# All warming matmuls taken out of a single-core transformer trunk in fp32

## What is computed

```python
for i in range(2):
    sh1, sc1, g1, sh2, sc2, g2 = split(silu(c) @ ada_w[i] + ada_b[i], 6)
    hm = rms_norm(x, gain[i, 0]) * (1 + sc1) + sh1
    mix = attention(hm) if i == 0 else mamba2_mixer(hm)
    x = x + g1 * mix
    hf = rms_norm(x, gain[i, 1]) * (1 + sc2) + sh2
    ffn = swiglu(hf) if i == 0 else moe_swiglu(hf)
    x = x + g2 * ffn
```

## Time and profile before

| | |
|---|---|
| median of 3 runs | 1727.41 us |
| the three runs | 1726.98, 1727.41, 1732.47 us |
| profiled execution | 1734.41 us |
| its span | 1732.6 us |
| granted TensorE clock, mean over the span | 0.983 |
| TensorE busy (share of the span) | 1661.9 us (96%) |
| VectorE busy | 1395.3 us (81%) |
| ScalarE busy | 1094.1 us (63%) |
| read from HBM | 495.78 MB, 287 GB/s over the span |

### The profile page before, as it was taken

One profiled execution on the slowest core, in us unless ns is written; L12 is line 12 of the kernel. 1 busy time (PEld: TensorE's weight loads), 2 busy tenths in 40 slices (PEclk: granted clock), 3 DMA queues, 4 the chain that ended last, 5 costly groups with the idle time before them and its releaser, 6 DMA issues.

```text
span 1732.6 us, 25093 instructions
## 1 busy us (share of the span) xinstructions
PE 1661.9 (96%) x7709; PEld 1308.4 (76%) x7709; DVE 1395.3 (81%) x1557; ACT 1094.1 (63%) x1333; POOL 0.2 (0%) x4
## 2 busy tenths in 40 slices
PE   7888999999999989899999999999999999999996
PEld 2735777778778768588888888888888888888884
DVE  2565887776567685799898998998998998998996
ACT  2544444433365663577777777777877787787773
POOL 0000000000000000000000000000000000000000
PEclk9989999999999989899999999999999999999998
DMA  9667597876545215299999998998999999999991
GB/s 358 239 236 273 218 358 274 279 257 217 175 125 179 85 39 157 68 372 374 346 354 365 346 361 335 383 358 329 387 361 341 364 365 337 362 375 342 354 375 72
DMA packets 206214, 497.94 MB, mean 287 GB/s; under 512 B 18155, under 2 KB 20508, under 8 KB 205992
## 3 DMA queue, kind: packets, MB, share of 16 engines
q1 hardware_dynamic: 206120, 496.91, 79.8%
HBM read 495.78 MB, written 1.07 MB: 287 GB/s over the span
## 4 chain that ended last, share of the span: by engine, by line
PE 86%; DVE 5%; ACT 3%; issue 2%; DVEq 0%; ACTq 0%
PE acc L1565 25%; PE acc L1572 25%; PE acc L1566 24%; PE xb L1854 2%; PE xb L1820 2%; PE xb L1602 1%; PE acc L1550 1%; PE acc L1665 1%; DVE cv L1332 1%; DVE w_lo L926 1%; PE acc L1948 1%; PE xb L1650 1%; PE xb L1843 1%; PE xb L1844 1%; PE xb L1872 0%
## 5 line engine op out<-in xcount | busy, mean ns | idle before, releaser
L926 DVE TENSOR_TENSOR w_lo<-raw,w_hi 128x1024 fp32r<-128x1024 f32 x832 | 993.7, 1223 | 167.3 <-ACT w_hi L575 142.3
L575 ACT ACTIVATE w_hi<-raw 128x1024 fp32r<-128x1024 f32 x832 | 864.8, 1058 | 306.3 <-PE acc L1572 283.0
L1565 PE MATMUL acc<-w_hi,g_hi 128*128 128x512 f32 x896 | 354.3, 395 | 1.0 <-DVE g_lo L1511 1.0
L1566 PE MATMUL acc<-w_hi,g_lo 128*128 128x512 f32 x896 | 349.0, 390 | 0.0
L1572 PE MATMUL acc<-w_lo,g_hi 128*128 128x512 f32 x896 | 276.6, 390 | 0.2 <-DVE w_lo L926 0.2
L1572 PEld LDWEIGHTS acc<-w_lo,g_hi 128*128 128x128 f32 x896 | 168.0, 188 | 36.3 <-DVE w_lo L926 0.8
L1565 PEld LDWEIGHTS acc<-w_hi,g_hi 128*128 128x128 f32 x896 | 168.3, 188 | 34.5 <-issue 1.1
L1565 PE MATMUL acc<-w_hi,a_hi 128*128 128x512 f32 x464 | 185.2, 399 | 8.9 <-DVE a_lo L976 4.6
L1566 PEld LDWEIGHTS acc<-w_hi,g_lo 128*128 128x128 f32 x896 | 168.4, 188 | 33.2
L1566 PE MATMUL acc<-w_hi,a_lo 128*128 128x512 f32 x464 | 181.7, 392 | 0.0
L1565 PE MATMUL acc<-w_hi,e_hi 128*128 128x512 f32 x448 | 177.9, 397 | 0.0
(11 more groups left out here) (254 smaller groups left out, 1469.2 us busy)
## 6 DMA issues: line engine op xcount, KB each, us to landing
raw<-in_moe_w_gu SPq DMA_DIRECT2D x448, 512.0 KB, 6.0
raw<-in_moe_w_down SPq DMA_DIRECT2D x224, 512.0 KB, 5.3
raw<-in_ada_w SPq DMA_DIRECT2D x96, 512.0 KB, 6.1
raw<-in_ffn_w_gu SPq DMA_DIRECT2D x56, 512.0 KB, 5.8
raw<-in_ssm_w_in SPq DMA_DIRECT2D x40, 512.0 KB, 4.7
raw<-in_ffn_w_down SPq DMA_DIRECT2D x28, 512.0 KB, 5.0
raw<-in_ssm_w_out SPq DMA_DIRECT2D x16, 512.0 KB, 4.2
raw<-in_attn_w_qkv SPq DMA_DIRECT2D x12, 512.0 KB, 15.1
```

Of the source, the lines that this page charges most:

```text
L575: act.activation(w_hi[:, w % SPLIT, :], raw[:, no % RAW, :], ACT.Copy).then_inc(hi_ready, 1)
L926: dve.tensor_tensor(w_lo[:, w % SPLIT, :], raw[:, no % RAW, :], r32(w_hi[:, w % SPLIT, :]), ALU.subtract).then_inc(raw_used, 1)
L1565: pe.matmul(o, l_hi[:, k, rows_], hi[:, col:col + HALF], start=new, stop=False)
L1566: pe.matmul(o, l_lo[:, k, rows_], hi[:, col:col + HALF], start=False, stop=False)
```

## The change

All six counts become 0, so `keep_warm` issues nothing in any of the eight places. TensorE's program has 3008 rows in place of 3016; the waits for PSUM buffers that stand ahead of `keep_warm`, and the programs of the other engines, are the same.

```diff
-WARM_FIRST, WARM_NORM, WARM_SSD, WARM_Y, WARM_MASK, WARM_ROUTE = 3, 9, 5, 4, 2, 3
+WARM_FIRST, WARM_NORM, WARM_SSD, WARM_Y, WARM_MASK, WARM_ROUTE = 0, 0, 0, 0, 0, 0
```

## The result

The changed kernel took 1750.24 us in the median of 4 runs (1747.68 to 1752.08), against 1729.87 us for the kernel before (1726.98 to 1732.47, 4 runs). The ratio is 1.0117, with a 95% interval of 1.0099 to 1.0136: slower by 1.2%. The profiled execution took 1752.08 us.

A forecast was written before the change was run, and what follows sets the result against it. TensorE, nearly always granted full clock, was taken to bound the kernel. Terms 5.6 + 2.0 + 3.8 + 1.1 + 0.9 + 4.6 = 18.0 us, put on the 1727.4 median, gave 1745.4 us, range 1736 to 1754.

The forecast's parts named there:

- What is saved: At all emptied waits: removed passes free no time, except 0.4 us at the routing, where they delay the gather.
- The unit price: At each cold start: 4.2 us at half clock once dense products begin, a loss of 2.1 us.
- norm1, norm2: Transposes at half delay the first product by 0.7 us, then a 2.1 us cold start: 2.8 us each.
- norm0: Clock falls near the wait's end, transposes still run in full: 2.0 us lost, bounds 0 and 3.1.
- The scan: First unit runs at half throughout, 4.7 us more, 0.9 made up: 3.8 us, bounds 1.7 and 4.7.
- Gated norm: Transposes 0.7 us later, then 2.1, but 1.7 already lost before: 1.1 us, bounds 0 and 2.8.
- norm3: First transposes 0.7 us later, clock already at half afterwards, 0.2 added: 0.9 us, bounds 0 and 1.5.
- Routing: Gather at half, 2.5 us including the 0.4 saved, then first expert's cold start 2.1: 4.6 us.
- The smaller price: Whole kernel: clock returns faster or lost time is made up, 8.5 us more, 1736 us; chance 0.12.
- nothing: Whole kernel: clock does not fall or returns within the first product, 1727 us; chance 0.07, shared with a cancellation.
- stay cold: Scan: small products at half never bring the clock back, all eight units run at half, 1773 us; chance 0.05.
- Rival 3: Norm waits and routing: passes begun at low clock last twice as long, so removal is faster, 1724 or 1716; chance 0.04.

The follow-up runs named there:

- Parts and whole: Four runs against the kernel before, passes removed at the norms, scan, mask and routing, norm0 and gated norm: 1.0033, 1.0023, 1.0026, 1.0032; whole change 1.0117.
- the two light forms: Kernel before with its 44 warming matmuls using only 8 identity columns (ratio 0.9993), or only 8 rows of identity and constants (ratio 1.0209).
- 3.5 alone: Kernel before without warming passes at norm1, norm2 and norm3 only: 1737.19 against 1729.97 us, ratio 1.0033.
- 2.0 alone: Kernel before without warming passes at norm0 and ahead of the gated norm's transposes only: 1735.65 against 1729.26 us, ratio 1.0032.
- 5.0 alone: Kernel before without warming passes ahead of the first scan unit only: 1735.08 against 1729.97 us, ratio 1.0023.
- the run with 8 rows: Kernel before with warming matmuls using 8 rows of identity and constants, 8 partitions read, 128 written: 1766.04 against 1729.26 us, ratio 1.0209.
- the last version of all: Kernel before plus warming matmuls: three behind norm3's first transposes, two behind the gated norm's, three ahead of the last scan unit: 1728.74 against 1731.63 us, ratio 0.9986.
- The run with twelve passes: Kernel before with twelve warming matmuls in place of nine at norm1, norm2 and norm3: 1737.79 against 1731.63 us, ratio 1.0053.
- that with five: Kernel before with five warming matmuls in place of nine at norm1, norm2 and norm3: 1739.24 against 1731.63 us, ratio 1.0043.

## Why the prediction was right

The forecast was 18.0 us more, 1745.4 in the median; measured were 20.4 us between the medians and 1750.24, inside the range of 1736 to 1754. Part of the distance lies in the reference: with one more run the median of before became 1729.87. The mechanism and the total were right; the terms were less so, and their errors cancel in part. Step by step:

- **What bounds.** TensorE, and its clock: right. Parts and whole add up, and the two light forms show that the clock is the cause.
- **What is saved: nothing, and 0.4 at the routing.** Right for the norms. At the routing 0.2 us was saved behind `pick`, but the five counting products (lines 1991 to 1995) that make VectorE's input stand 0.43 us apart instead of 0.22 with the clock down, which makes `pick` 1.0 us later. The prediction had priced the gather and the tiles at half and passed over these.
- **The unit price, 4.2 us at half behind the first dense product, 2.1 lost.** Right in the mean, but not the same at each place. The clock behind the first dense product of norm0, norm2, the gated norm and the first expert:

```profile
39.81:46.20 6.39, 6.39 (x20) 5.17 (x21) 2.32 (x3) 0.14 (x1) 0.00 (x0) 0.53 1.04 391
459.09:462.50 3.41, 3.41 (x9) 2.72 (x10) 2.42 (x4) 0.00 (x0) 0.00 (x0) 0.54 1.03 422
655.90:660.10 4.20, 4.20 (x10) 3.37 (x11) 4.20 (x5) 0.00 (x0) 0.00 (x0) 0.50 0.64 219
741.43:745.70 4.27, 4.27 (x10) 3.37 (x11) 4.27 (x5) 2.00 (x2) 0.00 (x0) 0.52 0.40 124
```

  With norm1 this makes about 6.0, 6.0, 3.1, 4.2 and 4.1 us at half, 4.7 in the mean. From the first product to the first behind the second transposes it took 6.41, 6.46, 5.08 and 5.62 us at norm0, norm1, norm2 and the gated norm, where 3.63 or 3.64 is the time in full; so 2.8, 2.8, 1.4 and 2.0 us were lost, and 1.9 in the first expert's first two tiles: 2.2 in the mean. That one price would fit both long and short ones was a simplification, and that they average out is luck.
- **norm1, norm2: 2.8 each.** Norm1 3.6 (3.5 alone); norm2 2.0, of which 0.7 is the transposes, as forecast, and 1.4 the products.
- **norm0: 2.0.** 2.7, and 2.0 alone.
- **The scan: 3.8.** 4.2, and 5.0 alone, of which 0.8 belongs to the last unit. The argument that the small products at half don't bring the clock back and that one whole unit is paid was right: the third unit is 4.9 us later relative to the first. Of that 0.5 is made up by the last unit and 0.7 by the gated norm, close to the 0.9 forecast.
- **Gated norm: 1.1.** 0.8.
- **norm3: 0.9.** 0.2. The transposes cost 0.7, but the router's last products ran in full in this execution, which gave most of it back.
- **Routing: 4.6.** 5.1, made up of 0.8 from the counts to the gather (1.0 lost at the counts, 0.2 saved), 2.9 from there to the first tile, and 1.4 up to the ninth tile; of the 1.9 us lost in the first two tiles the kernel before lost 0.5 itself a little later, in part waiting for `w_lo`.
- **The rivals.** The smaller price, nothing, and faster are out by the interval. The scan did not stay cold: its second unit was at full pace. Rival 3 did not occur here, but its mechanism is real, as the run with 8 rows shows.
- **The rule** of under 1% for coming up to the full clock, from the Trainium skill, page "TensorE: Matmul & The Clock Gate", section "What's actually happening", does not hold for this change as a whole: 1.17%, though the interval, 0.99 to 1.36, just touches 1. Read as the price of one ramp it agrees: the largest single place cost 5.1 us, 0.3%.

The forecast for the profiled execution, 1752.4, met 1752.08 by cancellation, which is luck: norm0, norm1, the scan and the routing came out 2.4 us above their terms together, and norm2, the gated norm and norm3 1.8 below; the rest of the table is 0.9 shorter, nearly all of it in the stretch up to the end.

The scatter between executions, 4 to 10 us in every kernel here, comes in good part from half-clock stretches between the first product of the query/key/value projection and that of the output projection. Over that part, the profiled execution of the kernel before and that of the last version of all, which issue the same instructions up to there:

```profile
39.91:150.84 110.93, 93.62 (x509) 53.91 (x509) 68.45 (x123) 51.05 (x125) 0.00 (x0) 0.92 0.71 256
```

```profile
40.18:143.81 103.63, 86.08 (x508) 51.28 (x508) 68.41 (x123) 51.02 (x125) 0.00 (x0) 1.00 0.74 270
```

7.3 us lie between them, at a mean clock of 0.92 and 1.00. The run with twelve passes, the same up to there as well, took 106.97 us at 0.97, that with five 112.68 at 0.91. So single profiled executions can't be compared by their whole spans, which is why the parts above are compared stretch by stretch. What makes the clock fall there in one execution and not in the next stays open.

## What to carry to other kernels

Count TensorE's idle time on a chain over other engines twice: once for itself, and once for the half clock that may follow it, which here cost 2 to 5 us at most of the waits, and under 1 at the gated norm and norm3, where the kernel before had part of the loss already. It was paid nearly in full because TensorE bounded the next stage. A wait has to be filled almost to its end: with nine matmuls the clock held over the 0.7 to 0.95 us left idle ahead of norm2, the gated norm and the scan; with five, and 3.26 us left at norm1, it did not, and the whole time was not told from that with none; twelve cost their overhang. And look at what small serial work stands between the wait and the dense products (transposes, counts, gathers), for it too runs at half.

## What was not expected of the hardware

Passes that kept TensorE busy without a gap did not hold the clock when they read 8 partitions (mean clock 0.64 over norm1's wait), while the same number of passes that read 128 and wrote 8 held it at 1.00. The router's products, which write 8 partitions too and behind which the clock was back, had pointed the same way. The penalty of this filler, which does not hold the clock, is larger than that of no filler: 36 us against 20.
